# A two-layer trunk's PEER mixer: u-blocks first, then v-blocks, and the prompt tile's expert rows fetched by index

## What is computed

```
def _peer(h, w_q, sub_keys, u_tab, v_tab):
    ...
    s1, i1 = lax.top_k(s[:, :, 0], PK_TOPK)
    s2, i2 = lax.top_k(s[:, :, 1], PK_TOPK)
    ...
    top_s, pos = lax.top_k(cand_s, PK_TOPK)
    idx = jnp.take_along_axis(cand_i, pos, axis=-1)
    gate = jax.nn.softmax(top_s, axis=-1).astype(h.dtype)
    def one(args):
        xb, ib, gb = args
        act = jax.nn.gelu(jnp.einsum("thkd,td->thk", u_tab[ib], xb)) * gb
        return jnp.einsum("thk,thkd->td", act, v_tab[ib])
```

## Time and profile before

| | us |
|---|---|
| median of 3 runs | 2977.23 (2976.36 to 2979.71) |
| span of the profiled execution | 2974.3 |
| TensorE busy in it | 2890.6 (97%) |
| VectorE busy | 1837.4 (62%) |
| ScalarE busy | 1067.7 (36%) |
| GpSimd busy | 97.2 (3%) |
| DMA | 543.11 MB, mean 183 GB/s |
| layer 1: hidden and v-blocks in turn | from 2200 to 2656 |
| layer 1: v-blocks alone | from 2656 to 2944 |

### The profile page before, as it was taken

One profiled execution on the slowest core, in us unless ns is written; L12 is line 12 of the kernel. 1 busy time (PEld: TensorE's weight loads), 2 busy tenths in 40 slices (PEclk: granted clock), 3 DMA queues, 4 the chain that ended last, 5 costly groups with the idle time before them and its releaser, 6 DMA issues. The chain is left out here.

```text
span 2974.3 us, 41189 instructions
## 1 busy us (share of the span) xinstructions
PE 2890.6 (97%) x16921; PEld 2600.1 (87%) x16921; DVE 1837.4 (62%) x3483; ACT 1067.7 (36%) x1626; POOL 97.2 (3%) x66
## 2 busy tenths in 40 slices
PE   8998899999999999999999889999999999999998
PEld 6997689999999999888879679999999999987886
DVE  3348687788444444466676559978944444446667
ACT  3434333355333333222243643345533333322222
POOL 1001200000000000000012002000000000000001
PEclk9999899999999999999999989999999999999999
DMA  8634674477734443366643134346773444426563
GB/s 291 217 115 160 215 255 165 156 286 295 276 135 163 152 156 135 110 215 230 216 164 107 51 115 135 123 165 259 305 291 136 143 154 165 143 84 238 206 238 141
DMA packets 208794, 543.11 MB, mean 183 GB/s; under 512 B 8032, under 2 KB 173280, under 8 KB 185824
## 3 DMA queue, kind: packets, MB, share of 16 engines
q1 hardware_dynamic: 207472, 539.93, 50.4%
q10 hardware_dynamic: 816, 0.48, 0.1%
q0 software_dynamic: 320, 0.07, 0.0%
HBM read 458.52 MB, written 81.92 MB: 182 GB/s over the span
## 5 line engine op out<-in xcount | busy, mean ns | idle before, releaser
L1358 PE MATMUL hidden_ps<-h_hi,u_hi 128*128 128x384 f32 x2016 | 682.7, 339 | 2.6 <-issue 1.6
L1358 PE MATMUL hidden_ps<-h_hi,u_lo 128*128 128x384 f32 x2016 | 675.5, 335 | 0.0
L1358 PE MATMUL hidden_ps<-h_lo,u_hi 128*128 128x384 f32 x2016 | 674.8, 335 | 0.0
L2014 PE MATMUL out_ps<-v_hi,act_hi 128*128 128x512 f32 x1488 | 584.0, 392 | 0.1
L2014 PE MATMUL out_ps<-v_hi,act_lo 128*128 128x512 f32 x1488 | 582.5, 391 | 0.0
L2014 PE MATMUL out_ps<-v_lo,act_hi 128*128 128x512 f32 x1488 | 581.7, 391 | 0.0
L2137 DVE TENSOR_TENSOR v_lo<-v_slot,v_hi 128x1024 fp32r<-128x1024 f32 x248 | 303.9, 1226 | 426.3 <-ACT v_hi L2064 426.3
L2064 ACT ACTIVATE v_hi<-v_slot 128x1024 fp32r<-128x1024 f32 x248 | 262.8, 1060 | 719.2 <-PE out_ps L2014 713.2
L1358 PEld LDWEIGHTS hidden_ps<-h_hi,u_hi 128*128 128x128 f32 x2016 | 378.8, 188 | 8.9 <-issue 4.7
L1358 PEld LDWEIGHTS hidden_ps<-h_lo,u_hi 128*128 128x128 f32 x2016 | 378.8, 188 | 4.2
L1358 PEld LDWEIGHTS hidden_ps<-h_hi,u_lo 128*128 128x128 f32 x2016 | 378.4, 188 | 0.0
(11 more groups left out here) (485 smaller groups left out, 3746.0 us busy)
## 6 DMA issues: line engine op xcount, KB each, us to landing
u_slot<-in_peer_u SPq DMA_DIRECT2D x64, 2048.0 KB, 7.8
v_slot<-in_peer_v SPq DMA_DIRECT2D x64, 2048.0 KB, 7.9
spread_gates<-spread SPq DMA_DIRECT2D x24, 2048.0 KB, 7.2
w_ring<-spread_gates SPq DMA_DIRECT2D x64, 768.0 KB, 9.9
...
```

Source lines behind the costliest of these rows:

```text
L1358: mm = pe.matmul(PH_[:, b, 0:T], u[:, b, k * P:(k + 1) * P], x[:, k, :], start=(k == 0 and part == 0), stop=(k == KB - 1 and part == 2))
L2014: mm = pe.matmul(PO[:, t, c, :], a[:, t * P:(t + 1) * P], x[:, c * CH:(c + 1) * CH], start=(o == 0 and part == 0), stop=(o == N_KEYS - 1 a ...
```

## The change

Hidden blocks 0 to 63 (not 71) are computed in `peer_front`, hidden blocks 64 to 127 alone in the first part of `peer_experts`, all for 384 tokens as before. All of them go to DRAM (tensor `hidden`); those from 64 on are multiplied by the gates before that (`gate_hidden`), for tiles 1 and 2 alone. Then all 128 v-blocks follow in order, for tiles 1 and 2: 12 matmuls each.

Dense gates are made for tiles 1 and 2 alone: 16 steps for 24. For the prompt tile `row_numbers` (DVE) works out two tables of indices. In the v stage GpSimd issues for each of the 128 prompt tokens two indirect DMAs: `row` fetches the token's 128 picked v rows (128 x 4 KB, 512 KB) into one of 11 slots, and `picks` fetches its 128 gelu values (4 bytes each) from `hidden`. For four tokens at a time (a quad, 32 of them) DVE multiplies the picked values by the gates into columns (`act_columns`), and TensorE sums the rows (`row_sums`): 2 halves x 4 tokens fp32 matmuls with 32 stationary columns, each token in its own group of 32 output rows of `out_ps`, accumulated over all quads. A quad's sums stand behind v-block 8, 11, 15 and so on up to 122.

```diff
-        WD = nc.dram_tensor("spread_gates", [P, T // TG, N_KEYS, TG], F32).ap()
+        WD = nc.dram_tensor("spread_gates", [P, TD // TG, N_KEYS, TG], F32).ap()
...
-        EARLY = 72
+        EARLY = 64
         SEL_N = 2 * PH
-        TAIL_N, GATE_N, LAST_N = (11, 4, 4, 4), T // 16, 5
+        TAIL_N, GATE_N, LAST_N = (11, 4, 4, 4), TD // 16, 6
         IN_TURN = [2 if h % 6 == 2 else 1 for h in range(GATE_N)]
...
-                        if n == gates_at + 5:
-                            sp.wait_ge(v_gate, TT)
-                            sp.wait_ge(gate_rows, 4)
-                            sp.dma_start(V0.rearrange("p j n -> p (j n)"), I["peer_v"][l, EARLY // JC].rearrange("p j d -> p (j d)")).then_inc(v0_in, 16)
...
+                        if t == 0:
+                            act.activation(PICK0[:, :, :], PT[:, 0:3 * P].rearrange("p (k t) -> p k t", k=3), ACT.Copy).then_inc(pk_taken, 1)
+                            return
...
+                    def row_numbers():
+
+                        dve.wait_ge(pk_taken, 1)
+                        first, second = PICK0[:, 1, :], PICK0[:, 2, :]
+                        v.mark(dve.tensor_copy(IDIG[:, :], second))
+                        v.mark(dve.scalar_tensor_tensor(ACT0[:, :], second, 32.0, first, ALU.mult, ALU.add))
+                        v.wait()
+                        v.mark(dve.scalar_tensor_tensor(first, first, float(N_KEYS), second, ALU.mult, ALU.add))
+                        v.mark(dve.tensor_single_scalar(IDIG[:, :], IDIG[:, :], 3, ALU.bitwise_and))
+                        v.wait()
+                        v.mark(dve.scalar_tensor_tensor(IDXG[:, :], first, float(T), iota, ALU.mult, ALU.add))
+                        v.mark(dve.scalar_tensor_tensor(ACT0[:, :], IDIG[:, :], -31.75, ACT0[:, :], ALU.mult, ALU.add))
+                        v.wait()
+                        v.seq(dve.tensor_scalar(IDXV[:, :], ACT0[:, :], 4.0, float(l * N_KEYS * N_KEYS), ALU.mult, ALU.add))
...
+                VH, VL = (M.at(n, M.phase + o, [P, 2, D], F32R) for n, o in (("v_hi", 24576), ("v_lo", 32768)))
+                A = M.at("act", M.phase + 40960, [P, 2, TD])
+                AH, AL = (M.at(n, M.phase + o, [P, 2, TD], F32R) for n, o in (("act_hi", 43008), ("act_lo", 45056)))
+                HV = M.at("hidden_in", M.phase + 47104, [P, 2, JC, TD])
+                SDW = M.at("act_columns", M.phase + 67584, [P, 4, 4, 63])
+                S = (None, M.at("ln_stats", M.phase + 71616, [P, 2, 6]), M.at("ln_moments", M.phase + 71680, [P, TT, 4]))
+                SLOT_AT = (*(M.phase + 55296 + 4096 * n for n in range(3)), M.picks, M.u + 36864, M.u + 40960, M.u + 45056,
+                           *(20480 + 4096 * n for n in range(4)))
+                RING, FREE = len(SLOT_AT), 4
+                ROWS = [M.at(f"row_slot{n}", o, [P, D]) for n, o in enumerate(SLOT_AT)]
+                LN = M.at("ln_rows", 12288, [P, 2, D])
...
-                ORDER = [*range(EARLY // JC, CHUNKS), *range(EARLY // JC)]
-                AT = {c: m for m, c in enumerate(ORDER)}
-                BLOCKS = [JC * c + j for c in ORDER for j in range(JC)]
-                PLACE = {n: o for o, n in enumerate(BLOCKS)}
+                CHUNKS, FIRST_U = N_KEYS // JC, EARLY // JC
+                GATED = CHUNKS - FIRST_U
+                QUADS = P // 4
+                QUAD_AFTER = [8 + i * (LATE - 10) // (QUADS - 1) for i in range(QUADS)]
+                assert QUAD_AFTER[-1] < LATE
...
                     load_w(1)
-                    load_hidden(0)
-                    load_hidden(1)
+                    for m in range(2, GATED + 2):
+                        if FIRST_U + m < CHUNKS:
+                            load_u(FIRST_U + m)
+                        load_w(m)
+                        spill(FIRST_U + m - 2)
+                        if m < 4:
+                            load_v(m - 2)
+                            load_hidden(m - 2)
                     for m in range(2, CHUNKS):
-                        if ORDER[m] >= EARLY // JC + 2:
-                            load_u(ORDER[m])
                         load_v(m)
-                        load_w(m)
-                        if 2 <= ORDER[m] < EARLY // JC:
-                            load_hidden(ORDER[m])
+                        if m < FIRST_U:
+                            load_w(GATED + m)
+                        load_hidden(m)
...
+                    def row_sums(i):
+                        pe.wait_ge(acts_made, i + 1)
+                        for j in range(4 * i, 4 * i + 4):
+                            pe.wait_ge(slot_in[j % RING], 16 * (j // RING + 1))
+                        for c in range(2):
+                            for g in range(4):
+                                mm = pe.matmul(PO[TG * g:TG * g + TG, 0, c, :], SDW[:, i % 4, g, 31 - i:63 - i],
+                                               ROWS[(4 * i + g) % RING][:, c * CH:(c + 1) * CH],
+                                               start=(i == 0), stop=(i == QUADS - 1), skip_group_check=True)
+                        mm.then_inc(rows_summed, 1)
+
+                    for n in range(EARLY + 1, N_KEYS):
+                        hidden_products(pe, PH_, UH, UL, HH, HL, n, uh, ul, g_done, h_done)
                     for o in range(LATE):
-                        if BLOCKS[o + 1] >= EARLY:
-                            hidden(BLOCKS[o + 1])
                         pe.wait_ge(a_done, o + 1)
                         pe.wait_ge(vl, o + 1)
-                        for t in range(TT):
+                        for t in range(1, TT):
                             mm = outs(o, t)
                         mm.then_inc(o_done, 1)
+                        if o in QUAD_AFTER:
+                            row_sums(QUAD_AFTER.index(o))
...
+                    for n in range(EARLY, N_KEYS):
+                        gelu(n)
+                        if n + 2 < N_KEYS:
+                            high_part(n + 2)
+                        if n in (N_KEYS - 12, N_KEYS - 11):
+                            v_part(n - N_KEYS + 12)
+                    for o in range(2, N_KEYS):
...
+                    def row(j):
+                        t = token(j // 4, j % 4)
+                        if j >= RING:
+                            pool.wait_ge(rows_summed, (j - RING) // 4 + 1)
+                        pool.indirect_dma_start(ROWS[j % RING], None, table,
+                                                bass.IndirectOffsetOnAxis(ap=IDXV[:, t:t + 1], axis=0)).then_inc(slot_in[j % RING], 16)
+
+                    def picks(i):
+                        if i >= 4:
+                            pool.wait_ge(acts_made, i - 3)
+                        for g in range(4):
+                            t = token(i, g)
+                            pool.indirect_dma_start(ACT0[:, t:t + 1], None, hidden,
+                                                    bass.IndirectOffsetOnAxis(ap=IDXG[:, t:t + 1], axis=0)).then_inc(pick_in[i % 4], 16)
+
+                    pool.memset(SDW, 0.0).then_inc(zeroed, 1)
+                    for j in range(FREE):
+                        row(j)
+                    pool.wait_ge(h_done, N_KEYS)
+                    for n in range(2):
+                        pool.wait_ge(hg_out[n], 16 * (CHUNKS // 2))
+                    picks(0)
+                    for j in range(FREE, RING):
+                        row(j)
+                    picks(1)
+                    picks(2)
+                    at = RING
+                    for i in range(QUADS):
+                        while at < min(P, RING + 4 * i + 4):
+                            row(at)
+                            at += 1
+                        if i + 3 < QUADS:
+                            picks(i + 3)
...
+                    def gate_hidden(n):
+                        m, j = divmod(n - EARLY, JC)
+                        dve.wait_ge(g_done, n + 1)
+                        if j == 0:
+                            dve.wait_ge(w_in[m % 2], 16 * (m // 2 + 1))
+                        g = groups(HG[:, n // JC % 2, n % JC, P:T])
+                        dve.tensor_tensor(g, g, W[m % 2][:, :, j * TG:(j + 1) * TG], ALU.mult).then_inc(gated, 1)
...
                     def weigh(o):
-                        b, m, n = o % 2, o // JC, BLOCKS[o]
-                        if n >= EARLY:
-                            dve.wait_ge(g_done, n + 1)
-                            g = G[:, n % 2, :]
-                        else:
-                            at, j = divmod(n, JC)
+                        c, j = divmod(o, JC)
+                        m = GATED + c
+                        if j == 0:
+                            dve.wait_ge(hg_in[c % 2], 16 * (c // 2 + 1))
+                        a = HV[:, c % 2, j, :]
+                        if o < EARLY:
                             if j == 0:
-                                dve.wait_ge(hg_in[at % 2], 16 * (at // 2 + 1))
-                            g = HG[:, at % 2, j, :]
```

(45 more changed lines are left out.)

150 lines of the change are left out of this document (79 added, 71 removed).

## The result

The changed kernel takes **2813.4 us** (median of 4 runs, 2808.1 to 2815.9), the kernel before 2976.8 beside it: a ratio of 0.9451, 95% interval 0.9437 to 0.9464. The forecast was 2835 us, range 2768 to 3006. The profiled execution has a span of 2811.7 us against 2974.3, 162.6 less.

The account below looks back on a forecast made before the run. TensorE bounds the kernel, with the ACT/DVE chain exactly under it. Per layer 54 (v stage 514 to 460) + 16 (front) + 1 (tail, start) = 71 us; 2974.3 - 142 = 2832, plus 2.9: 2835 us, range 2768 to 3006.

Parts of the forecast that it names:

- rival D: Row sums' four groups take turns on TensorE: 7.6 us a quad, stage 614, 3140 us; chance 0.04.
- The recurrence: V stage: each block starts at the later of TensorE's pace and the two-blocks-back chain; 435 us for 124 blocks with quads.
- the chain: ACT and DVE steps from block o-2's last product to block o's first: 3.96 us before, 3.62 (3.17 from block 64) after.
- Casts that wait for GpSimd: V stage: one DVE cast a block meets GpSimd's indirect DMAs, 0.4 us on the chain, recurrence from 435 to 449 us.
- Late v slots: V stage: v slots asked for some 15 us ahead land late and hold ACT; 11 us added, ends 0 and 60.
- The start: Start of the v stage: perhaps 2 us gained back; tail and start together left at +1 us a layer.
- The first has seven blocks: V stage: picks are issued three quads (some 40 us) ahead, the first quad's only seven blocks; said to cost nothing.
- the engines need 95% of the stage, so slots come late: V stage: DMA engines need 427 us of 449, 95% where they had 62%, making v slots late.
- the point from which it decides: GpSimd bounds the layer from 2.08 us an indirect DMA on, from (514 + 19) / 256.
- rival A: Only TensorE and the chain bind; DMA engines keep up, casts meet nobody: stage 435, 2782 us; chance 0.18.
- B: DMA engines bind outright, everything at 335 GB/s: 520 us a stage, 2951 us; chance 0.14 with the cases between.
- C: GpSimd and DVE exclude each other on one read port, 2.4 us a block on the chain: 3006 to 3037 us; chance 0.16.

Follow-up runs that it names:

- e5_sums_of_two: Changed kernel with only the first and a last quad of row sums, 30 of 32 left out with their picks and rows; 2707.2 us.
- e9_swap_in_before: Kernel before, with DVE doing the next block's cast and subtraction ahead of the low-part subtraction in v-blocks standing alone; 2965.2 us, ratio 0.9964.
- e4_no_rows: Changed kernel without the row DMAs after the first 11 of a layer, row sums using old rows; 2812.6 us.
- e1_swap: Changed kernel with DVE doing a block's cast and subtraction while ACT makes its high part, before the low-part subtraction; 2807.9 us.
- e7_picks_twice: Changed kernel with every picks DMA issued twice, 384 indirect DMAs a layer instead of 256; 3028.9 us.

## Why the prediction came out

**Right.** The products that go away (from 18 to 12 a block) and the front's 8 gate steps, 15 us measured for 15.7. The row sums: 1.85 us a quad with four groups side by side, taken as 2.0; rival D is out. The recurrence itself: 14.12 us for four blocks and a quad where it had 14.06, 13.67 in the second half (2593.36 to 2607.03) where it had 13.61. The row sums cost less than their own time (e5_sums_of_two). The kernel before had the chain just under TensorE (e9_swap_in_before).

**Mis-sized, and in which step.** The stage was put at 460 us and took 450:

- Casts that wait for GpSimd: 0.4 us a block on the chain, 14 us a layer. The casts took 0.33 and 0.29 us where 0.29 is undisturbed, 0.04 us in each of 64 blocks, some 3 us a layer. I had read one cast of 0.55 us across a direct DMA in the earlier trace rows and let every meeting cost half an instruction. The Trainium skill, "SBUF — State Buffer", section "Who interferes with whom", says that a cast can run in a 2-port mode and that in such a mode DVE and GpSimd block each other for the whole instruction. Here GpSimd was in an indirect DMA about 60% of the time and the casts came through nearly untouched; which part of such an instruction holds a port, if any, no run shows.
- Late v slots: 11 us. e4_no_rows, with its DMA share of 0.61, has 449.0 and 449.4 us for the two stages, the changed kernel 453.2 and 447.1, about 1 us more on the mean. That comparison flatters the changed kernel, for the start of e4_no_rows was some 3 us longer. Block by block, layer 0 of the changed kernel loses 7 us at blocks 48 and 49 by one late load of hidden values: DVE waited 3.89 us for it, TensorE idled 3.75 us and then ran its next products at a granted clock of 0.50. Layer 1 loses next to nothing in this way. So late inputs cost 3 to 4 us a layer, and not by v. The step "the engines need 95% of the stage, so slots come late" was the wrong one.
- The start: a gain of 2 us was put down. The recurrence with 1.9 us a quad gives 432 us. Against it the changed kernel is 8.5 and 9.6 us late at block 16 in the two layers (64.5 and 65.5 us into the stage where the recurrence has 56.0), and after that it loses 6 us more, a little at a time. "The first has seven blocks" was true for the picks of quad 0, which were 0.73 us late; those of quad 1 stood behind seven rows on GpSimd, a queue that I had counted only for its total.
- GpSimd: 1.1 us an instruction was right (1.07 to 1.15), but the 0.30 us between two was left out. It cost no time here, but made the margin smaller. It was occupied some 80% of the stage, not 63%, and the point from which it decides is an estimated 1.68 us with the gap, not 2.08.

So the stage of 460 us comes down by the casts (14), the late slots (11) and the quads (3, taken as 2.0 us) to 432, and goes up again by the start (9), the slow loss (6) and the late load of layer 0 (7) to 453 and 447. The forecast's number lies 22 us from the measured one, rival A's 31, but the mechanism is A's: TensorE and the chain bind, the DMA engines keep up but for that load, the casts meet nearly nobody. That the forecast came nearer than A is luck: it had two terms of 25 us a layer that were hardly there, and they were partly made up by the start and the slow loss, which were missing. A with the start's 9 us a layer would have said 2800. B is out for this kernel (e4_no_rows) but lies directly behind it: e1_swap, which takes away the chain, gains 5 us where the chain alone was worth 58. C was out by the subtractions' 0.43 us; e7_picks_twice shows where GpSimd would have decided, by its own time and not by a port.

Two numbers of the prediction have no row behind them. B's price took 335 GB/s for everything, which no row showed; the changed kernel then moved 364 over 160 us. And the range's lower end of 2768 was called TensorE alone with cheap row sums, which would be 342 + 32 x 1.7 = 396 us a stage and 2703 in all; 2768 belongs to a stage of 428, which the recurrence gives for 1.8 us a quad. Neither changes where the measured time lies in the range.
